# The mixing layer's head exchanges, issued by ScalarE instead of GpSimd

## What is computed

```python
def _token_mixing(u, w_in, decay_fwd, decay_bwd, rel_bias, w_ret_out, w_na_out, w_out, pos):
    rq, rk, rv, rg, nq, nk, nv, g_ret, g_na = jnp.split(u @ w_in, points, axis=-1)
    q = _rotary(heads(rq, RET_QK_DIM), pos)
    k = _rotary(heads(rk, RET_QK_DIM), pos) * (RET_QK_DIM ** -0.5)
    y = _bidirectional_retention(q, k, heads(rv, RET_V_DIM), decay_fwd, decay_bwd)
    y = y * lax.rsqrt(jnp.mean(y * y, axis=-1, keepdims=True) + RMS_EPS)
    y_ret = (jax.nn.silu(rg) * y) @ w_ret_out
    y_na = _neighborhood_attention(na_heads(nq), na_heads(nk), na_heads(nv), rel_bias) @ w_na_out
    merged = jax.nn.sigmoid(g_ret) * y_ret + jax.nn.sigmoid(g_na) * y_na
    return merged @ w_out
```

## Time and profile before

| | |
|---|---|
| median of three runs | 1201.81 us |
| the profiled execution | 1207.52 us |
| its span (first to last instruction) | 1205.7 us |
| TensorE busy | 1189.4 us (99%) |
| VectorE busy | 952.8 us (79%) |
| ScalarE busy | 621.3 us (52%) |
| GpSimd busy | 108.7 us (9%) |
| mean granted TensorE clock | 0.997 |

### The profile page before, as it was taken

How to read it: one execution, slowest core, us unless ns; L and a number is a source line. 1 busy time by engine, 2 the same in 40 slices (tenths; PEclk the granted TensorE clock), 3 DMA queues, 4 the chain that set the end, 5 groups by cost and what they waited for, 6 DMA issues and landing times.

```text
span 1205.7 us, 14695 instructions
## 1 busy us (share of the span) xinstructions
PE 1189.4 (99%) x5718; PEld 976.5 (81%) x5718; DVE 952.8 (79%) x1380; ACT 621.3 (52%) x847; POOL 108.7 (9%) x163
## 2 busy tenths in 40 slices
PE   9999999989999999999999999999999999999997
PEld 7888888878778888888887778888888778888885
DVE  7799868876866689888785768898998878765656
ACT  7345337455774363434465667443446566643441
POOL 2110130220330011000000000000100000000000
PEclk9999999999999999999999999999999999999999
DMA  9999895874685489999557637788856754566540
GB/s 321 350 335 322 309 301 189 271 228 149 194 234 178 153 296 354 310 331 315 174 202 247 174 107 266 272 303 282 309 194 225 244 174 140 176 217 218 187 162 35
DMA packets 168500, 284.79 MB, mean 236 GB/s; under 512 B 23520, under 2 KB 97712, under 8 KB 168432
## 3 DMA queue, kind: packets, MB, share of 16 engines
q1 hardware_dynamic: 148368, 213.93, 53.6%
q0 software_dynamic: 19904, 69.86, 17.3%
q10 hardware_dynamic: 160, 0.07, 0.0%
HBM read 275.66 MB, written 8.18 MB: 235 GB/s over the span
## 4 chain that ended last, share of the span: by engine, by line
PE 66%; DVE 5%; ACT 3%; DMA 3%; issue 2%; SPq 1%; POOL 0%; DVEq 0%
PE ps L552 16%; PE ps L553 15%; PE ps L554 15%; PE ps L881 7%; PE ps L885 4%; ACT hi_w L1207 2%; PE ps L752 2%; DVE lo_w L1731 2%; DMA head_scratch<-area 1%; PE ps L803 1%; PE ps L758 1%; DMA area<-head_scratch 1%; PE ps L1094 1%; PE ps L631 1%; DMA w_raw<-in_moba_w_in 1%
## 5 line engine op out<-in xcount | busy, mean ns | idle before, releaser
L1731 DVE TENSOR_TENSOR lo_w<-w_raw,hi_w 128x2048 fp32r<-128x2048 f32 x194 | 440.7, 2285 | 64.6 <-ACT hi_w L1207 64.3
L1207 ACT ACTIVATE hi_w<-w_raw 128x2048 fp32r<-128x2048 f32 x195 | 369.9, 1915 | 57.6 <-DMA w_raw<-in_ffn_w_in 13.9
L552 PE MATMUL ps<-hi_w,xT 128*128 128x512 f32 x848 | 339.1, 400 | 0.0
L554 PE MATMUL ps<-lo_w,xT 128*128 128x512 f32 x848 | 331.0, 390 | 0.0
L553 PE MATMUL ps<-hi_w,xT 128*128 128x512 f32 x848 | 330.7, 390 | 0.0
L552 PEld LDWEIGHTS ps<-hi_w,xT 128*128 128x128 f32 x848 | 159.5, 188 | 36.6 <-issue 5.0
L552 PE MATMUL ps<-hi_w,hT_hi 128*128 128x512 f32 x480 | 188.4, 393 | 0.0
L554 PEld LDWEIGHTS ps<-lo_w,xT 128*128 128x128 f32 x848 | 159.3, 188 | 34.4
L553 PE MATMUL ps<-hi_w,hT_lo 128*128 128x512 f32 x480 | 187.1, 390 | 0.0
L554 PE MATMUL ps<-lo_w,hT_hi 128*128 128x512 f32 x480 | 186.9, 389 | 0.0
L553 PEld LDWEIGHTS ps<-hi_w,xT 128*128 128x128 f32 x848 | 159.6, 188 | 31.0
(11 more groups left out here) (332 smaller groups left out, 1138.3 us busy)
## 6 DMA issues: line engine op xcount, KB each, us to landing
w_raw<-in_ffn_w_in SPq DMA_DIRECT2D x86, 512.0 KB
aux<-in_ada_w POOLq DMA_DIRECT2D x34, 1024.0 KB, 7.1
w_raw<-in_mlp_w_up SPq DMA_DIRECT2D x32, 1024.0 KB
w_raw<-in_mlp_w_down SPq DMA_DIRECT2D x32, 1024.0 KB
w_raw<-in_w_mix_in SPq DMA_DIRECT2D x26, 1024.0 KB
w_raw<-in_ffn_w_out SPq DMA_DIRECT2D x22, 1024.0 KB
area<-in_ada_w POOLq DMA_DIRECT2D x14, 1024.0 KB, 5.7
w_raw<-in_moba_w_in SPq DMA_DIRECT2D x12, 1024.0 KB
```

The costliest lines, as they stand in the source:

```text
L552: pe.matmul(dst, lhs_hi, rhs_hi, start=start, stop=False)
L554: return pe.matmul(dst, lhs_hi, rhs_lo, start=False, stop=stop)
L1207: act.activation(hi_w[:, ring_slot(u), :], w_raw[:, ring_slot(u), :], ACT.Copy).then_inc(w_hi, 1)
L1731: vec.tensor_tensor(lo_w[:, ring_slot(u), :], w_raw[:, ring_slot(u), :], hi_w[:, ring_slot(u), :].bitcast(F32), ALU.subtract).then_inc(w_l ...
```

## The change

The four exchanges of the mixing layer move from GpSimd's list to ScalarE's, and with them from GpSimd's software queue to ScalarE's own hardware queue. They get semaphores of their own, `mix_saved` and `mix_landed`. The writes of exchange n are issued in ScalarE's slot 2n + 3, before that slot's split, and the read in slot 2n + 4, behind `mix_out` and before the split. The number and the shapes of the transfers stay. The exchanges of `y_rows` stay on GpSimd, with their counts lowered by four.

```diff
@@ TensorE
             def ret_scores(h):
-                pe.wait_ge(head_landed, 2 * 16)
+                pe.wait_ge(mix_landed, 2 * 16)
...
             def na_scores_of(pair):
-                pe.wait_ge(head_landed, 4 * 16)
+                pe.wait_ge(mix_landed, 4 * 16)
@@ ScalarE
+            def mix_heads_save(n):
+                act.wait_ge(head_turned, n + 1)
+                for a in range(4):
+                    rows = slice(32 * a, 32 * a + 32)
+                    act.dma_start(head_dram[n].rearrange("y i k -> i y k")[:, :, rows],
+                                  turned[rows, :].rearrange("p (y j) -> p y j", j=32)).then_inc(mix_saved, 16)
+
+            def mix_heads_load(n):
+                act.wait_ge(mix_saved, 64 * (n + 1))
+                act.dma_start(mix_heads[n].rearrange("p (x n) -> p x n", n=P),
+                              head_dram[n].rearrange("(x b) i n -> (b i) x n", b=4)).then_inc(mix_landed, 16)
+
             u = U_MIX
             for slot in range(2 * N_MIX):
                 if slot % 2 == 0 and slot >= 2:
                     mix_out(slot // 2 - 1)
+                if slot in (3, 5, 7, 9):
+                    mix_heads_save((slot - 3) // 2)
+                if slot in (4, 6, 8, 10):
+                    mix_heads_load((slot - 4) // 2)
...
-                act.wait_ge(head_landed, 16 * 6)
+                act.wait_ge(head_landed, 16 * 2)
@@ VectorE
                     if n >= 1:
-                        vec.wait_ge(head_saved, 64 * n)
+                        vec.wait_ge(mix_saved, 64 * n)
                     vec.transpose(turned, stage[n % 2].rearrange("p t n -> p (t n)")).then_inc(head_turned, 1)
@@ GpSimd
-            def heads_exchanged(n, src, dst):
-                heads_saved(n, src)
-                pool.wait_ge(head_saved, 64 * (n + 1))
-                heads_loaded(n, dst)
...
             for h in range(2):
                 bias_of(h)
-            for n in range(4):
-                heads_exchanged(n, turned, mix_heads[n])
             for h in range(2, NA_H):
                 bias_of(h)
...
-            pool.wait_ge(head_saved, 64 * 6)
+            pool.wait_ge(head_saved, 64 * 2)
```

More of the change, by code:

```diff
@@ L332, in two_blocks_kernel @@
         head_turned, head_saved, head_landed = sem("head_turned"), sem("head_saved"), sem("head_landed")
+        mix_saved, mix_landed = sem("mix_saved"), sem("mix_landed")
         late_saved, late_landed = sem("late_saved"), sem("late_landed")
```

## The result

| | before | after |
|---|---|---|
| median, runs on the same chip | 1202.45 us (6 runs, 1201.54 to 1204.09) | 1208.67 us (6 runs, 1205.82 to 1209.30) |
| the profiled execution | 1207.52 us | 1209.06 us |
| its span | 1205.7 us | 1207.2 us |

The change makes the kernel slower: the ratio is 1.0048, with a 95% interval from 1.0037 to 1.0058. Between the medians it is 6.2 us, where the prediction had 1.4 us less and a range that ended 2.5 us short of the result.

The account below looks back on a forecast made before the run. The prediction took TensorE, 99% busy, as the bound, with 4.8 us to gain at its wait for exchange 1. Four write groups summing to 14.2 us left 15.6 - G = 1.4 us: 1201.81 to 1200.4 us, range 1196.9 to 1206.2.

Parts of the forecast that it names:

- gain that wasn't there: At the first ret_scores: removing the 3.3 us wait and the slow clock behind it could give at most 4.8 us.
- the two small waits: TensorE's forecast waits of 0.2 us for the read of exchange 1 and 2.1 us at ret_outputs(0) for mix_out(4).
- I take the difference as the same in both, since it lies in one stage.: The 1.4 us saved in the profiled execution (1207.52 us) was also taken off the timed median (1201.81 us).
- group 1: Four writes of exchange 1 on ScalarE's list, starting at 233.9, 1.3 us ahead of a weight issue: 2.9 us.
- Group 0: Four writes of exchange 0 on ScalarE's list, from 219.15, 0.85 us behind a weight issue: 4.6 us.
- TensorE's wait before slot 8: TensorE, ready at 240.5, waits for mix_out(2) to empty block 2 of PSUM until 241.6: 1.1 us.
- the second wait: TensorE waits 2.1 us for mix_out(4) before ret_outputs(0); a clock fall behind it would take 1.5 us.
- a clock of 0.50 anywhere in the stretch: Sign of a wrong forecast: the granted clock at its lower level; the forecast expected 1.00 around the first ret_scores.
- The read of exchange 1: Issued by ScalarE at 241.6, landing after 5.7 us at 247.3; the first ret_scores' wait shrinks from 3.3 to 0.2 us.
- Groups 2 and 3: Writes of exchanges 2 and 3 on ScalarE's list ahead of mix_out(4): 3.8 and 2.9 us.
- my third rival: ScalarE hands over transfers while its split ahead still runs, group 2 starting 1.8 us earlier: gain 3.2, 1198.6 us; chance 0.10.
- The rival on the other side: Long groups on ScalarE, 4.6 us or more each: 18.4 to 20.6 together, 1204.6 to 1206.8 us; chance 0.27.

Follow-up runs that it names:

- scores_free: Kernel before with ret_scores multiplying two position tables instead of the exchanged queries and keys, so it doesn't wait for the exchange; 1201.60 us, ratio 0.9995.
- two_on_act: Changed kernel with only exchanges 0 and 1 on ScalarE, 2 and 3 given back to GpSimd; 1204.61 us, ratio 1.0019.
- split_first: Changed kernel with each group of four writes moved behind its own slot's split on ScalarE; 1209.14 us, ratio 1.0055.
- big_pieces: Changed kernel with each write in 32 pieces of 4 KB instead of 1024 of 128 bytes, same bytes; 1202.19 us, ratio 0.9999.
- late_on_act: Changed kernel with exchanges 0 and 1 back on GpSimd and only 2 and 3 on ScalarE; 1208.96 us, ratio 1.0056.
- stall_only: Kernel before, transfers untouched, with ScalarE running five dependent copies behind each of the first two transpositions, in slots 3 and 5; 1208.88 us, ratio 1.0052.
- sync_writes: Kernel before with the 16 writes issued by SyncE on the weights' queue and the reads still by GpSimd; 1207.50 us, ratio 1.0035.
- stall_first: Kernel before with ScalarE held by five dependent copies in slot 3 only, nothing in slot 5; 1205.36 us, ratio 1.0028.
- stall_short: Kernel before with ScalarE held in slots 3 and 5 by three dependent copies each (3.25 us); 1204.70 us, ratio 1.0023.
- stall_second: Kernel before with ScalarE held by five dependent copies in slot 5 only, nothing in slot 3; 1201.98 us, ratio 0.9999.
- pool_writes: Changed kernel with the 16 writes back on GpSimd and only the four reads on ScalarE; 1204.11 us, ratio 1.0015.

## Why the prediction was wrong

That ScalarE's list is the place and that the loss arises in front of `mix_out` were right, and so was the chain up to `mix_out(2)`; one assumption and one size were wrong. Of the 8.3 us between 1200.4 and 1208.67, 4.2 are gain that wasn't there (4.8 - 0.6), 5.0 the larger wait before slot 8 with its slow clock, and 0.6 the median of before, which was 1202.45 in the runs beside after's; 2.3 go off for the two small waits that didn't come. That makes 7.5, and 0.8 are left open.

1. **The step that failed: "I take the difference as the same in both, since it lies in one stage."** The profiled execution was 5.7 us above the median of the runs shown, and I carried the saving of a wait of 4.8 us from the one to the other. The difference was in good part that wait itself. `scores_free` bounds what it is worth in the timed runs at 0.6 us, by the median. By my own sum, with 0.6 us to win and not 4.8, the forecast would have been a loss of 2.8 us. Both numbers stood in the tables before: 1207.52 beside 1201.81, with a single long wait in the profile. This alone turns the sign.
2. **The term that was mis-sized: group 1.** I put it at 2.9 us on ScalarE's list, on the ground that it starts 1.3 us ahead of a weight issue; it measured 5.46. The rows gave a band from 2.93 to 7.93, and the order of a weight issue didn't predict where in it a group falls: over four kernels (after, `two_on_act`, `split_first`, `big_pieces`) group 1 took 5.46, 2.36, 5.5 and, with big pieces, 2.4. I had read the hold as "a third write can't be handed over until the first two have been moved"; the runs show a long hold now at the second write, now at the third or fourth, and at times at none. Group 0 (4.6 forecast, 5.09) was nearly right.
3. **TensorE's wait before slot 8.** The chain gave 1.1 us; it was 4.5. Of the difference of 3.4, 2.6 are group 1, 0.5 group 0, and the rest small terms. With it comes the fall of the clock, 1.65 us more, which I had weighed only for the second wait. The form that the prediction called wrong, "a clock of 0.50 anywhere in the stretch", is what happened.
4. **The read of exchange 1** was to land with a wait of 0.2 us left; there was none, as TensorE came late itself. Nor did a read take the 8.04 us that I weighed beside it: they landed in 4.2 to 6.2.
5. **Groups 2 and 3.** I put them on the path with 3.8 and 2.9 us and a wait of 2.1 us at `ret_outputs(0)`. In the profile of after no wait is there. Two things hid it: TensorE is late by itself, and group 2 was handed over in 2.2 us beside running activations. This is the mechanism of my third rival, and it exists, though it wins nothing here. `late_on_act` shows that the place is real once the first wait is gone. The forecast had `mix_out(4)` end at 262.2, and it ended at 263.4; this nearness is luck in part, for a group 1 of 2.6 us more and a group 2 that hardly held the list cancelled each other.
6. **The rival on the other side** (long groups, 1204.6 to 1206.8) had the place and the kind of loss right, but not the sum: the four groups of after together take 15.9 us, hardly more than the 14.2 of the forecast and less than the rival's 18.4. It isn't the sum that decides but which group is long, and the rival's price held the same 4.8 us of gain and left out the clock.

The Trainium skill (Perfetto Trace Analysis, section on the hardware-issued DMA instruction) has the sequencer held until all descriptors are generated. The trace agrees on ScalarE's own queue so far as the list was held for 5.09 and 5.46 us by groups with 1024 pieces a write and for 1.86 and 2.43 us by groups with 32. The number of pieces alone doesn't give the time, though: groups of the same shape on ScalarE took from 2.2 to 7.0 us. I had cited the rule and then took a cheap case for group 1 all the same.

Waits of TensorE plus the slow stretch behind them give the timed loss within 0.8 us in most kernels: after 6.1 against 6.2; `stall_only` 4.8 + 2.2 = 7.0 against 6.6; `sync_writes` 3.7 + 1.8 = 5.5 against 5.2; `late_on_act` 4.5 + 2.9 (the time from `ret_outputs(0)` to the first product of slot 11 is 5.5 us instead of 2.6) = 7.4 against 7.1; `stall_first` 2.7 against 3.5; `stall_short` 2.2 against 2.8; `two_on_act` 3.0 against 2.3; `stall_second` and `big_pieces` none against 0.1 and -0.1; `pool_writes` 1.6 against 2.0, with the short waits behind the slots counted. `split_first` (4.5 against 7.0) doesn't fit.

No version here beats the kernel before. `scores_free` bounds what was there to be had at this place, at some 0.05%, and it leaves work out.

## What to carry to other kernels

When a profiled execution is some us longer than the timed ones, look whether its one long wait is that difference before counting the wait as a gain; a run without the wait tells. Handing many small pieces to a hardware queue holds the issuing engine for microseconds, and it counts for most in the list of an engine on which another one waits for its next input: the same 5.4 us cost 3.5 us in slot 3 and nothing in slot 5. Two overruns on one path aren't added: the first one gives the second its cover, and removing one alone can leave the loss whole, as taking exchanges 0 and 1 off ScalarE did (7.1 us lost against 6.2), where taking off 2 and 3 gave back about 4 of the 6.2 us.

## What the runs showed of the hardware

- Four writes of 1024 pieces of 128 bytes hold ScalarE for 2.2 to 7.0 us. Without a hold each takes 0.31 to 0.74 us. The held one is not always the third, as I had read from SyncE's rows: in after it was the third of group 0 (3.50 us) and the fourth of group 1 (3.73 us), and in `late_on_act` the second of group 3 (3.17 us).
- ScalarE hands transfers over while activations issued before them still run (writes at 249.08 and 250.04 of after beside the exponential at 249.08 and the split at 249.61), so the list is held only for what stands behind the transfers.
- The granted clock was 0.50 behind waits of TensorE of 3.3, 4.5, 4.5 and 4.8 us and also behind that of 3.7 us, for 3 us. Behind the one of 2.4 us it was 0.66 over 3 us. Behind waits of 0.9 to 1.8 us it stayed at 1.00.
